# Decay products of a chunked state-space scan: the masked logs as a rounded part and a rest, multiplied in fp32r instead of fp32

## The chip, the cores and the metric

One core of one Trainium2 chip runs the whole kernel. The metric is device time in microseconds, median of three runs. Five compute queues matter here: TensorE (PE, with its weight loads shown apart as PEld), VectorE (DVE), ScalarE (ACT), GpSimd (POOL), and the SyncE queue (SP), which issues most DMAs.

## The reference, cut to what matters

The model is one layer of a hybrid decoder: an input projection, a Mamba-2 branch (chunked scan), a short-convolution branch, a merge, and a mixture of experts. The change touches one intermediate of the scan, the decay matrix of a chunk:

```python
acum = jnp.cumsum(dt * a_neg.reshape(G, R), axis=2)
causal = jnp.tril(jnp.ones((chunk, chunk), dtype=bool))
seg = acum[:, :, :, None] - acum[:, :, None, :]
decay = jnp.exp(jnp.where(causal[:, :, None, None], seg, -jnp.inf))
cb = jnp.einsum('bclgn,bcsgn->bclsg', Cm, Bm)
wts = cb[..., None] * decay * dt[:, :, None]
y_diag = jnp.einsum('bclsgr,bcsgrp->bclgrp', wts, x)
```

`seg[l, s]` is the sum of `dt*a` over the tokens s+1 to l. There are 32 heads in 4 groups of 8, and 592 tokens (528 of the prompt with its meta tokens, 64 of eight short sample sequences).

## The kernel before

The 592 tokens stand as five tiles: four of 128 tokens and one of 80 (16 prompt tokens and the 64 sample tokens). After the short-convolution branch and its projection, a loop over the 4 groups (`for g`) does the scan. Each turn of it has these stages.

**Convolutions.** PE multiplies blocks of `w_in` (`pe_block`, L570 to L588: 48 fp32r matmuls a block, on a rounded and a rest half of weights and activations, 264 and 328 columns in turn). ACT copies a block's result into `raw` (L1566, L1567), DVE convolves it (L1147, L1149) into `cv`, ACT applies SiLU (L1545). Six such tiles c = 0 to 5 per group. POOL writes history columns into `raw` (L1791), saves its tails (L1799, L1800), and makes the rest half of each weight block (`split_lo`, L1736) two blocks ahead of its use.

**Token tiles i = 0 to 4.** PE transposes x (L678), multiplies B and C (L681) and transposes B (L682). Then, for each half q of the group's heads (4 heads):

- POOL's `decays(i, q)` (L1812 to L1820) writes `rbuf[q]`: the 0/1 mask `m_le` (rows not after the column) times the log decays `da` of 4 heads, broadcast to 128 x 512 (80 x 320 for tile 4). It first waits until the product that read the same buffer is done (`p_seg`).
- PE multiplies it by the strict mask `m_gt` into PSUM bank `pS` (L691). The trace shows each of these fp32 instructions as two records. It has waited for `s_r` (POOL's operand) and `s_exp` (ACT has read the bank's last content), so the second half starts only after the first half's exp.
- ACT writes the exp of the bank to `wts` (L1581), DVE multiplies it by the masked B-C product (L1180, both operands in SBUF).

PE goes on with C times the state (L697), the output products of the eight heads (L747, which waits for both L1180), the state's increment (L753) and a transpose back (L773). Parts of three z-gate blocks (`pe_block` with `part=0` or `part=1`) fill PE between those steps in tiles 0, 1 and 2: part 1 of a block behind L697, part 0 of the next ahead of the second L691 of tiles 1 and 2. Tiles 3 and 4 have none.

**Tile 4** holds the sample sequences. DVE's order there is L1164 and L1165 (x times dt, from PSUM), L1168 (a copy of `sdec`, SBUF to SBUF, 80 x 512), L1172 (mask of the B-C product, from PSUM). PE's L702 waits for L1168 and, through `s_cb`, for L1172; behind it on PE stand the transposes of the sample states (L713), their products (L722, L729), and then L747. POOL's `bmask` product (L1839, two inputs in SBUF) waits for the group's last L691, because it overwrites `rbuf`. POOL's L1846 follows, gated by L713.

The order on each engine is written out by hand; semaphores link the engines. POOL's order around tile 0 is: tail of convolution tile 5, `decays(0, 0)`, `decays(0, 1)`, the `split_lo` for block 8 (used in tile 1), `decays(1, 0)` and so on.

`da` itself is made once, before the loop (L1128), and multiplied by the masks for the cumulated sums (L657 to L661).

Of the kernel before, what the change touches and what calls it, by code (L numbers as in the profile page):

```python
# [4 lines left out]
F32 = mybir.dt.float32  # L5
F32R = mybir.dt.float32r
# [53 lines left out]
def build(nc, ins, outs):  # L60
    ctx = ExitStack()
    with ctx:
# [3 lines left out]
        def sb(name, shape, dt=F32):  # L66
            return ctx.enter_context(nc.sbuf_tensor(name, shape, dt))[tuple(slice(None) for _ in shape)]
# [4 lines left out]

        ident = sb("ident", [P, P])
        m_le = sb("m_le", [P, P])
        m_gt = sb("m_gt", [P, P])
        ones = sb("ones", [P, P])
        R4 = ROWS[4]
        m_le4 = sb("m_le4", [R4, R4])
        m_gt4 = sb("m_gt4", [R4, R4])
        m_blk4 = sb("m_blk4", [R4, R4])  # L80
        eps = sb("eps", [P, 1])
        stat = sb("stat", [P, 4, TILES])
# [3 lines left out]
        xtail = sb("xtail", [P, XT_TILES, TAIL])  # L86
        stail = sb("stail", [P, 8, STAIL])
        dt_, da = sb("dt", [P, TILES, HEADS]), sb("da", [P, TILES, HEADS])
        e_acum, dte, dec = (sb(n, [P, TILES, HEADS]) for n in ("e_acum", "dte", "dec"))
        sdec = sb("sdec", [R4, HEADS])  # L90
        dg = sb("dg", [P, GK, 2])
# [20 lines left out]
        def carve(at, shape, area=area, size=AREA):  # L112
            n = 1
            for s in shape:
                n *= s
            v = area[:, at:at + n]
            assert at + n <= size, (at, n)
            if len(shape) == 2:
                v = v.rearrange("p (a b) -> p a b", a=shape[0])
            if len(shape) == 3:  # L120
                v = v.rearrange("p (a b c) -> p a b c", a=shape[0], b=shape[1])
            return v, at + n
# [12 lines left out]
        wdt, o = carve(o, [8, HEADS])  # L135
        dtb, o = carve(o, [HEADS])
        ea, o = carve(o, [HEADS])
        dtw, o = carve(o, [6, TILES * HEADS])

        s_c, so = carve(0, [2, T])  # L140
# [10 lines left out]
        bT, o = carve(o, [T])  # L151
        cT, o = carve(o, [T])
        sz, o = carve(o, [GK, T])
        raw, o = carve(o, [2, XPAD])
        h0T_more, _ = carve(o, [2, GW])
        cv, o = carve(o, [2, XPAD])
        rbuf, o = carve(o, [2, 4 * P])
        bmask, _ = carve(o - 8 * P, [NSEQ, NST])
        wts, o = carve(o, [2, 4 * P])
        rms, _ = carve(o, [T])  # L160
# [430 lines left out]
        def _(pe):  # L591
# [75 lines left out]
            with pe.Fori(0, GROUPS) as g:  # L667
# [4 lines left out]
                pe.wait_ge(s_rm, g + 1)  # L672
                for i in range(TILES):
                    r = ROWS[i]
                    le, gt = (m_le, m_gt) if i < 4 else (m_le4, m_gt4)

                    for k in range(GK):
                        m = nc.tensor.transpose(pT[0:r, k * P:(k + 1) * P], xT[:, k, tok(i)], ident[:, :])  # L678
# [5 lines left out]
                    for q in range(2):  # L684
                        if q == 1 and 1 <= i < 3:
                            pe_block(pe, g_block(g, 7 + i), 7 + i, hT_hi, hT_lo, part=0)
                        pe.wait_ge(s_r, g * 10 + (2 * i + q + 1))
                        pe.wait_ge(s_exp, g * 10 + (2 * i + q + 1))
                        if q == 0:
                            pe.wait_ge(s_st, g * 6 + (i + 1))  # L690
                        nc.tensor.matmul(pS[0:r, 0:4 * r], gt[0:r, 0:r], rbuf[0:r, q, 0:4 * r],  # L691
                                         start=True, stop=True).then_inc(p_seg, 1)

                    pe.wait_ge(s_cb, g * 5 + (i + 1))
                    pe.wait_ge(s_bt, g * 5 + (i + 1))
# [317 lines left out]
        def _(dve):  # L1013
# [78 lines left out]
            def o1_turn(f):  # L1092
                use, _, a, ause = o1_block(f, 1)
                dve.wait_ge(o_sg, f + 1)
                dve.wait_ge(w_done, use + 2)
                a0, a1 = acc_parts(acc[a])
                g0, g1 = halves(sg[:, 0, :])
                m0, m1_ = halves(mT[:, bass.ds(f, 1), :].rearrange("p a b -> p (a b)"))
                v.tensor_tensor(m0, a0, g0, ALU.mult)
                v.tensor_tensor(m1_, a1, g1, ALU.mult).then_inc(acc_free[a], 1)  # L1100
                dve.wait_ge(acc_free[a], ause + 2)
                dve.sem_inc(o_m, 1)
# [4 lines left out]
            for h, bank_ in ((0, pY), (1, pS)):  # L1107
# [19 lines left out]
            dve.wait_ge(s_dta, 3)  # L1127
            v.scalar_tensor_tensor(da[:, :, :], dt_[:, :, :], -1.0, ea.unsqueeze(1).broadcast_to([P, TILES, HEADS]),  # L1128
                                   ALU.mult, ALU.mult).then_inc(s_dtv, 1)
            o1_turn(1)  # L1130
            dve.wait_ge(s_dta, 5)
            link(v.tensor_tensor(dte[:, :, :], dte[:, :, :], dt_[:, :, :], ALU.mult))
# [571 lines left out]
        def _(pool):  # L1704
# [12 lines left out]
            def select(out, in_, pattern, base, mult, op=ALU.is_ge, fill=0.0):  # L1717
                link(gp.affine_select(out=out, in_=in_, pattern=pattern, compare_op=op, fill=fill, base=base,
                                      channel_multiplier=mult))

            select(ident[:, :], ident[:, :], [[-1, P]], 0, 1, ALU.not_equal, 1.0)
            select(m_le[:, :], m_le[:, :], [[1, P]], 0, -1)
            select(m_gt[:, :], m_gt[:, :], [[-1, P]], -1, 1)
            blk = m_blk4[:, 0:LASTP]
            select(blk, blk, [[0, LASTP]], LASTP - 1, -1)
            blk = m_blk4[:, LASTP:R4].rearrange("p (s c) -> p s c", c=SLEN)
            select(blk, blk, [[-SLEN, NSEQ], [0, SLEN]], -LASTP, 1)
            select(blk, blk, [[SLEN, NSEQ], [0, SLEN]], LASTP + SLEN - 1, -1)
            select(m_le4[:, :], m_blk4[:, :], [[1, R4]], 0, -1)
            gp.affine_select(out=m_gt4[:, :], in_=m_blk4[:, :], pattern=[[-1, R4]], compare_op=ALU.is_ge, fill=0.0,  # L1730
                             base=-1, channel_multiplier=1).then_inc(consts, 1)

            def split_lo(where, b, ahead=2):
# [52 lines left out]
            with pool.Fori(0, GROUPS) as g:  # L1786
                def history(c):
                    hold(pool, s_cvd, g * 6 + (c + 1))
                    f = bass.ds(conv_tile(g, c), 1)
                    rows = raw[:, c % 2, XH + TP:XPAD].rearrange("p (s c) -> p s c", c=XROW)  # L1790
                    gp.tensor_copy(rows[:, :, 0:XH], xvec[:, f, 5:29].rearrange("p a (s c) -> p (a s) c", c=XH)  # L1791
                                   ).then_inc(s_hist, 1)

                def tail(c):
                    _, _, a, ause = g_block(g, c)
                    hold(pool, acc_free[a], ause + 2)
                    f = bass.ds(conv_tile(g, c), 1)
                    rows = raw[:, c % 2, XH + TP:XPAD].rearrange("p (s c) -> p s c", c=XROW)
                    gp.tensor_copy(xtail[:, f, 0:XH].rearrange("p a b -> p (a b)"), raw[:, c % 2, TP:TP + XH])  # L1799
                    gp.tensor_copy(xtail[:, f, XH:TAIL].rearrange("p a (s c) -> p (a s) c", c=XH), rows[:, :, SLEN:XROW]  # L1800
                                   ).then_inc(s_tail, 1)

                history(0)
                history(1)
                for c in range(6):
                    if c >= 1:
                        split_lo(g_block(g, c), c)
                        if c < 5:
                            history(c + 1)
                    tail(c)  # L1810

                def decays(i, q):  # L1812

                    r = ROWS[i]
                    le = m_le if i < 4 else m_le4
                    hold(pool, p_seg, g * 10 + (2 * i + q + 1))
                    gp.tensor_tensor(rbuf[0:r, q, 0:4 * r].rearrange("p (h c) -> p h c", h=4),  # L1817
                                     le[0:r, 0:r].unsqueeze(1).broadcast_to([r, 4, r]),
                                     da[0:r, i, bass.ds(g * HPG + 4 * q, 4)].unsqueeze(2).broadcast_to([r, 4, r]),
                                     ALU.mult).then_inc(s_r, 1)  # L1820

                decays(0, 0)
                decays(0, 1)
                split_lo(g_block(g, 6), 6)
                for i in range(1, TILES):
                    for q in range(2):
                        decays(i, q)
                    if i < 4:
                        split_lo(g_block(g, 6 + i), 6 + i)
                    if i == 1:  # L1830

                        hold(pool, s_silu, g * 6 + 8)
                        gp.tensor_copy(cmask[:, 0:LASTP], cT[:, 4 * P:TP])
                        diag = cmask[:, R4 + LASTP:R4 + LASTP + NSEQ * (R4 + SLEN)].rearrange("p (s c) -> p s c", c=R4 + SLEN)
                        gp.tensor_copy(diag[:, :, 0:SLEN], cT[:, TP:T].rearrange("p (s c) -> p s c", c=SLEN)).then_inc(s_cm, 1)

                hold(pool, s_bt, g * 5 + 5)
                hold(pool, p_seg, g * 10 + 12)
                gp.tensor_tensor(bmask[0:R4], btok[0:R4, 0, :].unsqueeze(1).broadcast_to([R4, NSEQ, NST]),  # L1839
                                 m_blk4[:, LASTP:R4:SLEN].unsqueeze(2).broadcast_to([R4, NSEQ, NST]), ALU.mult  # L1840
                                 ).then_inc(s_bm, 1)

                hold(pool, s_df, g + 1)
                hold(pool, p_h0, g * 8 + 8)
                for k in range(GK):
                    gp.tensor_tensor(hs[:, k], hs[:, k], df[:, k, :].unsqueeze(2).broadcast_to([P, NSEQ, NST]), ALU.mult  # L1846
                                     ).then_inc(s_hd, 1)
                hold(pool, p_yb, g * 4 + 4)
                hold(pool, p_hs, g * 4 + 4)
                split_lo(g_block(g, 10), 10)  # L1850
# [113 lines left out]
```

## Time and profile before

| | |
|---|---|
| median of three runs | 1428.02 us (1427.01 to 1428.05) |
| the profiled execution | 1430.2 us, span 1428.5 us, mean granted PE clock 0.953 |
| PE busy | 1324.7 us, 93% of the span |
| DVE busy | 567.5 us, 40% |
| POOL busy | 457.0 us, 32% |
| ACT busy | 377.9 us, 26% |
| L691, PE | 80 records for 40 instructions, 39.1 us |
| L1817, POOL | 40 instructions, 41.1 us |

The times are of one profiled execution. A busy share is of the whole span; the kernel has stages with different limits, so what a step is worth is read from the stage that it stands in. The group loop runs from about 324 us to about 830 us; the experts' stage begins after 940 us.

### The profile page before, as it was taken

The page shows a single profiled execution, that of the slowest core. Times are in us where ns is not written, and L with a number is a line of the kernel's source. Part 1 is how long each engine was busy: PE and PEld are TensorE (multiplying, and loading weights), DVE is VectorE, ACT ScalarE, POOL GpSimd, SP SyncE. Part 2 cuts the span into 40 slices and gives each one's busy share as a digit, 9 for nine tenths or more (in the row PEclk, how much of TensorE's full clock was granted, in tenths as well). Part 3 has the DMA queues.
Part 4 walks back from the last instruction along what each step waited for, and adds up shares of the span by engine and source line. Part 5 has one row for each costly group of instructions (what it writes and reads, how often), then busy time and mean ns, then how long its engine had stood idle before and what let it go on. Part 6 is the DMA issues. An engine that isn't in the chain of part 4 may idle for free.

```text
span 1428.5 us, 23149 instructions
## 1 busy us (share of the span) xinstructions
PE 1324.7 (93%) x9087; PEld 1027.3 (72%) x9087; DVE 567.5 (40%) x816; ACT 377.9 (26%) x574; POOL 457.0 (32%) x380
## 2 busy tenths in 40 slices
PE   4999999999989999998999999999987999999990
PEld 4999999999759877975987799994474444444430
DVE  5444441026566754955676550011153111111115
ACT  4212124344234324333342531210121111101102
POOL 5444432345333533533252454330002112122110
PEclk8999999999989999999999999999956999999995
DMA  5223222235107303520631222337612999999925
GB/s 144 75 75 87 74 68 65 78 84 151 48 13 186 109 0 110 132 65 7 182 104 43 81 74 75 89 104 267 279 49 67 363 368 374 370 360 376 378 97 203
DMA packets 179334, 209.75 MB, mean 147 GB/s; under 512 B 12988, under 2 KB 154428, under 8 KB 170896
## 3 DMA queue, kind: packets, MB, share of 16 engines
q1 hardware_dynamic: 167970, 187.97, 40.2%
q10 hardware_dynamic: 4134, 11.11, 2.2%
q0 software_dynamic: 7168, 9.81, 1.9%
q8 instruction: 44, 0.72, 0.2%
q14 instruction: 18, 0.14, 0.0%
HBM read 196.93 MB, written 32.34 MB: 160 GB/s over the span
## 4 chain that ended last, share of the span: by engine, by line
PE 75%; DVE 12%; issue 4%; ACT 3%; DMA 3%; SPq 1%; DVEq 1%; ACTq 0%; POOLq 0%; POOL 0%
PE acc L584 36%; PE pT L944 8%; PE acc L819 5%; PE pS L957 4%; PE acc L983 4%; DVE area L1149 4%; PE pY L747 2%; PE pS L991 2%; PE pS L691 2%; DMA ring<-in_w_in 1%; PE acc L920 1%; PE acc L713 1%; DVE big L1220 1%; PE pY L927 1%; PE pS L753 1%
## 5 line engine op out<-in xcount | busy, mean ns | idle before, releaser
L584 PE MATMUL acc<-h_parts,ring_parts 128*128 128x328 f32 (+1 forms) x3840 | 551.5, 305 | 12.6 <-DVE h_parts L1047 6.9
L584 PEld LDWEIGHTS acc<-h_parts,ring_parts 128*128 128x128 f32 x3840 | 537.7, 192 | 29.0 <-issue 28.2
L1736 POOL TENSOR_TENSOR ring_parts<-ring,ring_parts 128x1024 fp32r<-128x1024 f32 x104 | 263.2, 2531 | 419.3 <-ACT ring_parts L1468 419.3
L1468 ACT ACTIVATE ring_parts<-ring 128x1024 fp32r<-128x1024 f32 x104 | 110.0, 1058 | 371.1 <-PE acc L584 353.6
L944 PE MATMUL pT<-area,big 128*64 128x512 f32 x384 | 116.1, 611 | 0.2 <-ACT big L1665 0.2
L584 PE MATMUL acc<-u_parts,ring_parts 128*128 128x264 f32 (+1 forms) x640 | 109.4, 299 | 0.0
L584 PEld LDWEIGHTS acc<-u_parts,ring_parts 128*128 128x128 f32 x640 | 96.4, 188 | 0.0
L1149 DVE SCALAR_TENSOR_TENSOR area<-area,xvec 128x616 f32<-128x616 f32 x72 | 90.1, 1252 | 10.5 <-DVE area L1147 0.6
L944 PEld LDWEIGHTS pT<-area,big 128*64 128x64 f32 x384 | 35.5, 140 | 78.8 <-issue 78.8
L584 PE MATMUL acc<-area_parts,ring_parts 128*128 128x264 f32 (+1 forms) x512 | 91.1, 299 | 0.0
L584 PEld LDWEIGHTS acc<-area_parts,ring_parts 128*128 128x128 f32 x512 | 78.4, 188 | 0.0
L1890 POOL DMA_INDIRECT big<-h_rows,gid_main x16 | 16.7, 1043 | 161.9 <-DVE big L1351 107.6
L957 PE MATMUL pS<-area,big 128*32 128x256 f32 x768 | 58.5, 381 | 0.0
L983 PE MATMUL acc<-area,big 128*64 128x512 f32 x192 | 58.4, 598 | 0.0
L944 PE MATMUL pT<-ring,big 128*64 128x512 f32 x128 | 56.6, 595 | 0.0
L1677 ACT ACTIVATE big<-pT 128x256 f32<-128x256 f32 x16 | 6.1, 384 | 190.3 <-PE pT L944 190.3
L1817 POOL TENSOR_TENSOR area<-m_le,da 128x512 f32<-128x512 f32 (+1 forms) x40 | 41.1, 1031 | 47.1 <-PE pS L691 47.1
L1911 POOL DMA_INDIRECT y_tok<-big,sid_over x16 | 16.0, 998 | 125.1 <-DMA y_tok<-big,sid_main 125.1
L1240 DVE TENSOR_TENSOR area<-acc,area 128x528 f32<-128x528 f32 x8 | 5.7, 707 | 115.7 <-PE acc L584 115.7
L1382 DVE TENSOR_TENSOR big<-big,pT 128x256 f32<-128x256 f32 x16 | 6.7, 421 | 111.5 <-ACT big L1677 111.5
L691 PE MATMUL pS<-area,m_gt 128*128 128x512 f32 (+1 forms) x80 | 39.1, 570 | 12.8 <-ACT area L1581 12.8
L1180 DVE TENSOR_TENSOR area<-area 128x512 f32<-128x512 f32 (+1 forms) x40 | 35.8, 903 | 32.3 <-ACT area L1581 30.8
(332 smaller groups left out, 1708.5 us busy)
## 6 DMA issues: line engine op xcount, KB each, us to landing
ring<-in_w_in SPq DMA_DIRECT2D x80, 512.0 KB, 4.1
area<-in_w_gate SPq DMA_DIRECT2D x24, 1024.0 KB, 6.3
area<-in_w_up SPq DMA_DIRECT2D x24, 1024.0 KB, 9.3
area<-in_w_down SPq DMA_DIRECT2D x24, 1024.0 KB, 11.5
area<-in_state_ssm SPq DMA_DIRECT2D x16, 512.0 KB, 7.0
out<-area SPq DMA_DIRECT2D x16, 512.0 KB, 5.3
ring<-in_w_ssd_out SPq DMA_DIRECT2D x16, 512.0 KB, 4.2
ring<-in_w_gate SPq DMA_DIRECT2D x8, 1024.0 KB, 11.5
```

Source lines behind the costliest of these rows:

```text
L584: m = nc.tensor.matmul(acc[a][:, h, 0:n], w[s][:, k, :], x[:, k, h * HALF:h * HALF + n], start=first and k == 0 and w is w_hi and x is hi, ...
L691: nc.tensor.matmul(pS[0:r, 0:4 * r], gt[0:r, 0:r], rbuf[0:r, q, 0:4 * r], start=True, stop=True).then_inc(p_seg, 1)
L747: m = nc.tensor.matmul(pY[0:r, h * HD:(h + 1) * HD], wts[0:r, h // 4, (h % 4) * r:(h % 4 + 1) * r], xdt[0:r, i % 2, h * HD:(h + 1) * HD], ...
L819: m = nc.tensor.matmul(acc[n % 4 // 2][0:ROWS[i], n % 2, :], mT[:, k, tok(i)], wo[h][:, k, :], start=k == 0, stop=k == 7)
L944: m = nc.tensor.matmul(pT[main_of(j), :], xT_[:, k, main_of(j)], gate_up_w(2 * p + j, k), start=k == 0, stop=k == 7)
L957: m = nc.tensor.matmul(pS[over_of(q), 0:FE], xT_[:, k, at:at + OVER], wexp[(2 * p + j) % 4][n][:, k, :], start=k == 0, stop=k == 7)
L983: m = nc.tensor.matmul(acc[1][main_of(j), h, :], hT_main[:, ft, main_of(j)], wexp[(2 * p + j) % 4][2][:, ft, h * 512:(h + 1) * 512], start ...
L1149: x = v.scalar_tensor_tensor(o_, raw[:, c % 2, n:n + XCONV], w[:, 0, n:n + 1], o_, ALU.mult, ALU.add)
L1180: v.tensor_tensor(w, w, cbm[0:r, 0:r].unsqueeze(1).broadcast_to([r, 4, r]), ALU.mult).then_inc(s_w, 1)
L1468: a_.activation(w_hi[b % 2], w_raw[b % 2], ACT.Copy).then_inc(hi_done, 1)
L1736: gp.tensor_tensor(w_lo[b % 2], w_raw[b % 2], w_hi[b % 2].bitcast(F32), ALU.subtract).then_inc(lo_done, 1)
L1817: gp.tensor_tensor(rbuf[0:r, q, 0:4 * r].rearrange("p (h c) -> p h c", h=4), le[0:r, 0:r].unsqueeze(1).broadcast_to([r, 4, r]), da[0:r, i, ...
```

## The change

The operand `rbuf` becomes two fp32r operands. POOL multiplies the mask by `da` and writes it as fp32r (`r_hi`, the place of `rbuf`), and multiplies it by `da_lo`, the rest of `da` over its fp32r rounding (`r_lo`, in columns of `raw`). PE adds two fp32r products with an fp32r mask `m_gtr` in the place of one fp32 product. `da_lo` is made by two DVE instructions of 160 columns, once. For tile 0 the two low products wait for the group's convolutions, since `r_lo` lies in `raw`.

```diff
-        m_gt = sb("m_gt", [P, P])
+        m_gtr = sb("m_gtr", [P, P], F32R)
...
-                        pe.wait_ge(s_r, g * 10 + (2 * i + q + 1))
+                        pe.wait_ge(s_r, g * 20 + (4 * i + (2 * q + 2 if i else q + 3)))
                         pe.wait_ge(s_exp, g * 10 + (2 * i + q + 1))
...
-                        nc.tensor.matmul(pS[0:r, 0:4 * r], gt[0:r, 0:r], rbuf[0:r, q, 0:4 * r],
-                                         start=True, stop=True).then_inc(p_seg, 1)
+                        nc.tensor.matmul(pS[0:r, 0:4 * r], gt[0:r, 0:r], r_hi[q][0:r, 0:4 * r], start=True, stop=False)
+                        nc.tensor.matmul(pS[0:r, 0:4 * r], gt[0:r, 0:r], r_lo[q][0:r, 0:4 * r], start=False, stop=True
+                                         ).then_inc(p_seg, 1)
...
+            dve.wait_ge(s_dtv, 3)
+            link(v.tensor_copy(da_hi, da[:, :, :]))
+            v.tensor_tensor(da_lo[:, :, :], da[:, :, :], da_hi.bitcast(F32), ALU.subtract)
             o1_turn(1)
...
-                def decays(i, q):
+                HIGH, LOW = [(r_hi, da)], [(r_lo, da_lo)]
+
+                def decays(i, q, parts):
...
-                    gp.tensor_tensor(rbuf[0:r, q, 0:4 * r].rearrange("p (h c) -> p h c", h=4),
+                    for part, d in parts:
+                        gp.tensor_tensor(part[q][0:r, 0:4 * r].rearrange("p (h c) -> p h c", h=4),
...
-                decays(0, 0)
-                decays(0, 1)
+                decays(0, 0, HIGH)
+                decays(0, 1, HIGH)
+                hold(pool, s_cvd, g * 6 + 8)
+                hold(pool, s_tail, g * 6 + 8)
+                decays(0, 0, LOW)
+                decays(0, 1, LOW)
                 split_lo(g_block(g, 6), 6)
                 for i in range(1, TILES):
                     for q in range(2):
-                        decays(i, q)
+                        decays(i, q, HIGH + LOW)
```

## Rows read from the trace of the kernel before

**Rows 1.** Waits of PE, 320 to 830 us: in total, times, longest.

```profile
PE pS L691 <- ACT area L1581: 12.8, 12, 1.8
```

**Rows 2.** Busy time by engine in the stretch of group 1, clock, DMA.

```profile
440.90:566.00 125.10, 116.44 (x763) 97.50 (x762) 80.19 (x107) 45.74 (x76) 50.33 (x46) 0.99 0.32 88
```

**Rows 3.** Timeline, group 1, PE in tile 1: start, length, engine, line, records.

```profile
500.12 1.02 PE L691 MATMUL pS<-area,m_gt 128*128 128x512 f32 x2
500.98 1.02 PE L697 MATMUL pO<-area 128*128 128x512 f32 x2
...
505.45 1.89 PE L747 MATMUL pY<-area 128*128 128x64 f32 x16
```

**Rows 4.** Timeline, group 1, POOL in tile 1.

```profile
497.64 1.04 POOL L1817 TENSOR_TENSOR area<-m_le,da 128x512 f32<-128x512 f32 x1 [1.29 <-PE pS L691]
```

**Rows 5.** Timeline, group 1, last convolution and tile 0.

```profile
479.63 2.42 DVE L1149 SCALAR_TENSOR_TENSOR area<-area,xvec 128x616 f32<-128x616 f32 x2
...
484.12 1.02 PE L691 MATMUL pS<-area,m_gt 128*128 128x512 f32 x2
484.19 2.35 POOL L1736 TENSOR_TENSOR ring_parts<-ring,ring_parts 128x1024 fp32r<-128x1024 f32 x1 [3.81 <-ACT ring_parts L1468]
...
484.91 1.28 ACT L1581 ACT_TABLE_LOAD   x1
...
486.94 1.10 PE L691 MATMUL pS<-area,m_gt 128*128 128x512 f32 x2 [1.80 <-ACT area L1581]
```

**Rows 6.** Timeline, group 1, tile 3.

```profile
522.55 1.02 PE L691 MATMUL pS<-area,m_gt 128*128 128x512 f32 x2
...
523.83 0.72 POOL L1817 TENSOR_TENSOR area<-m_le,da 80x320 f32<-80x320 f32 x1 [1.60 <-PE pS L691]
...
524.35 1.10 PE L691 MATMUL pS<-area,m_gt 128*128 128x512 f32 x2 [0.78 <-ACT area L1581]
524.73 0.69 DVE L1180 TENSOR_TENSOR area<-area 128x512 f32<-128x512 f32 x1
...
525.71 0.72 POOL L1817 TENSOR_TENSOR area<-m_le,da 80x320 f32<-80x320 f32 x1 [1.16 <-PE pS L691]
526.11 0.86 DVE L1180 TENSOR_TENSOR area<-area 128x512 f32<-128x512 f32 x1 [0.69 <-ACT area L1581]
...
527.07 1.97 PE L747 MATMUL pY<-area 128*128 128x64 f32 x16 [0.77 <-issue]
```

**Rows 7.** Timeline, group 1, tile 4.

```profile
532.39 0.74 PE L691 MATMUL pS<-area,m_gt 80*80 80x320 f32 x2 [0.61 <-ACT area L1581]
532.93 0.41 DVE L1168 COPY area<-sdec 80x512 f32 x1
...
533.31 1.91 POOL L1839 TENSOR_TENSOR area<-area,m_blk 80x1024 f32<-80x1024 f32 x1 [6.89 <-PE pS L691]
533.55 1.06 PE L702 MATMUL pT<-ident,area 80*128 80x8 f32 x8 [0.42 <-DVE area L1172]
```

**Rows 8.** Timeline, narrow windows: DVE and POOL overlapping, twice.

```profile
307.65 2.12 DVE L1138 COPY dg<-dnv 128x8 f32 x1 [0.51 <-DVE big L1100]
...
307.31 2.40 POOL L1736 TENSOR_TENSOR ring_parts<-ring,ring_parts 128x1024 fp32r<-128x1024 f32 x1 [2.78 <-ACT ring_parts L1468]
...
477.91 1.57 DVE L1149 SCALAR_TENSOR_TENSOR area<-area,xvec 128x616 f32<-128x616 f32 x1
...
477.79 1.04 POOL L1817 TENSOR_TENSOR area<-m_le,da 128x512 f32<-128x512 f32 x1
```

**Rows 9.** L713 in groups 1 and 2; the stretch 661 to 662 us.

```profile
534.46 1.94 PE L713 MATMUL acc<-ident,area 128*128 128x128 f32 x16
...
659.57 3.60 PE L713 MATMUL acc<-ident,area 128*128 128x128 f32 x16
...
661.00:662.00 1.00, 1.00 (x7) 1.00 (x6) 0.07 (x1) 0.74 (x2) 0.00 (x0) 0.50 0.00 0
```

**Rows 10.** Timeline, DVE, the step behind the decay logs.

```profile
222.61 0.71 DVE L1099 TENSOR_TENSOR big<-acc,area 128x528 f32<-128x528 f32 x1 [6.24 <-PE acc L584]
```

More of the change, by code:

```diff
@@ L78, in build @@
         m_le4 = sb("m_le4", [R4, R4])
-        m_gt4 = sb("m_gt4", [R4, R4])
+        m_gtr4 = sb("m_gtr4", [R4, R4], F32R)
+        m_gt, m_gt4 = m_gtr.bitcast(F32), m_gtr4.bitcast(F32)
         m_blk4 = sb("m_blk4", [R4, R4])
@@ L88, in build @@
         dt_, da = sb("dt", [P, TILES, HEADS]), sb("da", [P, TILES, HEADS])
+        da_lo = svec.rearrange("p a b -> p (a b)").rearrange("p (i h) -> p i h", h=HEADS)
         e_acum, dte, dec = (sb(n, [P, TILES, HEADS]) for n in ("e_acum", "dte", "dec"))
@@ L137, in build @@
         ea, o = carve(o, [HEADS])
+        da_hi = area_parts[:, o:o + TILES * HEADS].rearrange("p (i h) -> p i h", h=HEADS)
         dtw, o = carve(o, [6, TILES * HEADS])
@@ L153, in build @@
         sz, o = carve(o, [GK, T])
+        r_lo = [area_parts[:, o + XPAD * q + 5 - q:o + XPAD * q + 5 - q + 4 * P] for q in range(2)]
         raw, o = carve(o, [2, XPAD])
@@ L156, in build @@
         cv, o = carve(o, [2, XPAD])
-        rbuf, o = carve(o, [2, 4 * P])
+        r_hi = [area_parts[:, o + 4 * P * q:o + 4 * P * (q + 1)] for q in range(2)]
+        o += 8 * P
         bmask, _ = carve(o - 8 * P, [NSEQ, NST])
@@ L674, in _ @@
                     r = ROWS[i]
-                    le, gt = (m_le, m_gt) if i < 4 else (m_le4, m_gt4)
+                    gt = m_gtr if i < 4 else m_gtr4
                     for k in range(GK):
@@ L1722, in _ @@
             select(m_le[:, :], m_le[:, :], [[1, P]], 0, -1)
-            select(m_gt[:, :], m_gt[:, :], [[-1, P]], -1, 1)
+            select(m_gtr[:, :], m_gt[:, :], [[-1, P]], -1, 1)
             blk = m_blk4[:, 0:LASTP]
@@ L1729, in _ @@
             select(m_le4[:, :], m_blk4[:, :], [[1, R4]], 0, -1)
-            gp.affine_select(out=m_gt4[:, :], in_=m_blk4[:, :], pattern=[[-1, R4]], compare_op=ALU.is_ge, fill=0.0,
+            gp.affine_select(out=m_gtr4[:, :], in_=m_blk4[:, :], pattern=[[-1, R4]], compare_op=ALU.is_ge, fill=0.0,
                              base=-1, channel_multiplier=1).then_inc(consts, 1)
@@ L1816, in decays @@
                     hold(pool, p_seg, g * 10 + (2 * i + q + 1))
-                    gp.tensor_tensor(rbuf[0:r, q, 0:4 * r].rearrange("p (h c) -> p h c", h=4),
-                                     le[0:r, 0:r].unsqueeze(1).broadcast_to([r, 4, r]),
-                                     da[0:r, i, bass.ds(g * HPG + 4 * q, 4)].unsqueeze(2).broadcast_to([r, 4, r]),
-                                     ALU.mult).then_inc(s_r, 1)
-                decays(0, 0)
-                decays(0, 1)
+                    for part, d in parts:
+                        gp.tensor_tensor(part[q][0:r, 0:4 * r].rearrange("p (h c) -> p h c", h=4),
+                                         le[0:r, 0:r].unsqueeze(1).broadcast_to([r, 4, r]),
+                                         d[0:r, i, bass.ds(g * HPG + 4 * q, 4)].unsqueeze(2).broadcast_to([r, 4, r]),
+                                         ALU.mult).then_inc(s_r, 1)
+                decays(0, 0, HIGH)
[4 more added lines that the diff above has]
+                decays(0, 1, LOW)
                 split_lo(g_block(g, 6), 6)
```

## The prediction, made before the changed kernel was run

> **What bounds the kernel now.** I read the busy shares first, then the stages by windows, then PE's waits in the group loop, and last the timeline of one group, because every edit but one lies in that loop. A turn of the loop takes about 125 us and PE is busy 116 of it [rows 2]; in its token tiles PE runs nearly without a gap, so what it saves there comes off the time, while the convolutions are a chain of DVE's that starts at the end of the turn before and moves with it. PE's only large wait at the changed line is for the exp of the first half of the heads: 12.8 us in 12 times, which are tiles 0, 3 and 4 of four groups [rows 1]. Tiles 1 and 2 have a z-gate block between the two L691 and do not wait. All of this lies in group 1 as in the other three, to within some hundredths of a microsecond until L702; I give group 1 and multiply by four.
>
> **PE's work at L691.** The pair of records holds PE for 500.98 - 500.12 = 0.86 us [rows 3]. For fp32r, the z-gate block between L697 and L747 gives the cadence: its 24 matmuls of 328 columns run from 500.98 + 0.86 = 501.84 to 505.45, 0.150 us each [rows 3]; that is 328 columns at 2.4 GHz (0.137) and 0.013 more, with a weight load for each. So 512 columns cost 0.213 + 0.013 = 0.226, the pair of products 0.45, and each L691 of 512 columns gets shorter by 0.40 us. In tile 4 the fp32 pair streams 320 columns in 0.53 us (the same 1.67 ns a column), the fp32r pair in 2 x 0.147 less the last overhead = 0.28, so 0.25 less. Forty instructions save 32 x 0.40 + 8 x 0.25 = 14.8 us of PE's work; what follows is how much of it arrives.
>
> **Tile 0: 0.4 us a group.** The first L691 (484.12) gains nothing: its exp follows a table load that runs from 484.91 to 486.19 whatever PE does [rows 5]. The second one (486.94) is followed by PE work without a gap: 0.40. The low products wait for the last convolution, which ends at 479.63 + 2.42 = 482.05; with an estimated 0.3 us from semaphore to start the one that PE waits for is there at 482.35 + 1.04 = 483.4, ahead of 484.12 [rows 5]. That cover is 0.7 us. Behind them on POOL stands the `split_lo` that started at 484.19 [rows 5]; the second low product ends at 484.4, so it moves 0.2 us, and its block is needed in tile 1 after 496 us.
>
> **Tiles 1 and 2: 0.8 us each.** PE is never idle there, so both L691 count: 4 x 0.40 = 1.6 us. POOL now has two products of 1.04 us in place of one; it starts the ones for tile 2 at 497.64, 12 us before they are used, with a gap behind them until 501.40 [rows 4]. What they delay on DVE (L1180 in tiles 1 and 2) has over 2 us of slack before L747.
>
> **Tile 3: 0.4 us, between -0.1 and 1.0.** Here L691, exp, L691, exp, L1180, L747 is one chain, and by itself it would give 0.8. But POOL and DVE exclude each other on SBUF, as the next part shows, and POOL's work doubles here. Shifted: the first L691 ends 0.4 earlier, so POOL's two products for tile 4 run from 523.43 (was 523.83) to 524.87. DVE's first L1180, ready at 524.73, gets through at 524.88 and ends at 525.42, as before (524.73 + 0.69) [rows 6]. POOL's next product is ready at 524.92, waits for it, and runs to 526.0; the second L1180, ready at 525.3, streams behind it and ends at 526.56 against 526.97. L747 starts 0.1 later, so at 526.66, 0.4 earlier than 527.07 [rows 6]. If DVE gets in first it is 1.0, if both products go ahead of it -0.1.
>
> **Tile 4: minus 1.6 us.** This is where the chain turns. L691 is not on the path here: L702 waits for DVE's L1164, L1165, L1168, L1172 [rows 7], which hang on the tile before, so the saved 0.5 us of PE brings nothing. But they release `bmask` (L1839) earlier. The second L691 starts 0.25 earlier and is 0.25 shorter, so L1839 starts at 533.31 - 0.51 = 532.80. DVE's L1168 starts at 532.93 [rows 7]. Before, the copy was 0.38 us ahead; now POOL is 0.13 us ahead, for 1.91 us.
> What that costs is in two pairs of rows. A copy of 8 columns took 2.12 us where a POOL product (307.31 + 2.40 = 309.71) had started before it and ended 0.06 before its end; and an L1149 that started at 477.91, 0.12 us after a POOL product of the very kind of the change (477.79 + 1.04 = 478.83), ended at 479.48, its 616 columns after the product's end [rows 8]. So the later one waits for the whole instruction, and a lead of 0.12 us has decided. L1168 would stream from 532.80 + 1.91 = 534.71 to 534.98, 1.64 us after its present end of 533.34, and L702 and everything behind it move by as much. Bounds: 0 (the copy first) and 1.7. I take 1.64 by the nearest row, the L1149 with a lead of 0.12.
> The page "SBUF — State Buffer" of the Trainium skill, section "Who interferes with whom", has the same: an exclusive lock, held for the whole instruction by whoever issues first. The other reading of a slow DVE row would be that both go on at a reduced rate (the copy at a third of its rate: 1.2 us in place of 0.41, and a loss of 0.8 a group); by that reading the sum below would be 3.4 us better, by the page it stands.
>
> **The clock.** The state transposes behind L702 took 1.94 us in group 1 and 3.60 in group 2, where the granted clock was 0.50, the lower level of 1.2 GHz [rows 9]; groups 0 and 2 have such a passage there, groups 1 and 3 not, 1.66 us each. The longer idle time of PE ahead of them (from about 532.5 to 535.2) can bring it to the others. Bounds: -3.3 us (gone from two groups) to +3.3 (in all four). I take one group more, +1.66, since what precedes a fall is idle time and there is now more of it.
>
> **What costs nothing.** The two DVE instructions for `da_lo` (160 columns) stand after the `s_dtv` step that PE waits for and before an `o1_turn` for which DVE waits 6.24 us in the trace [rows 10]; without that cover, below 1 us once, or up to 2.4 behind a POOL product as in [rows 8]. The mask in fp32r is written by the same instruction. The semaphore counts double without further instructions. Groups are coupled through DVE, the SP queue (state stores, then the next weight block) and ACT; all of them start from the end of tile 4, so a shift there passes on whole. The experts' loads start after all of it and move with it.
>
> **The sum.** Per group 0.4 + 1.6 + 0.4 - 1.64 = 0.76 us less, 3.0 us in four, and 1.66 given back to the clock: 1.4 us less. The profiled execution took 1430.2 us (span 1428.5), so it would take 1428.8; the median shown is 2.2 us below the profiled one, so the time to expect is 1428.0 - 1.4 = 1426.6 us.
>
> **The rivals.** *The copy goes first (0.27).* If L1168 takes its ports before L1839, nothing is lost in tile 4 and the gain is 2.4 a group, 9.6 us: 1418.4. For it: the margin of 0.13 us is a difference of worked-out times, and L1168's start overlaps the end of L1165, so it may ask earlier than its start. Against: the row with a lead of 0.12.
> *The clock takes more than is saved (0.17), the slower side.* Mechanism: PE idles 2.7 us ahead of L713 in each group, the clock falls there each time and stays low through the state products (L722) as well. Price: 1.66 in each of the two groups without it now, and about as much again in each group for the second half of that stage: 3.3 + 6.6 - 3.0 = 6.9 at the most, 3 to 4 if only some of it: about 1432. It decides as soon as the clock costs more than 0.76 us a group on average above today. For it: PE's gap grows from 0.6 + 0.4 to 2.7 us. Against: in group 1 gaps of the same stage passed at full clock. The page "TensorE: Matmul & The Clock Gate" of the Trainium skill, section "What's actually happening", says that the clock is granted by how busy PE has recently been. By that rule a longer gap speaks for the fall in each group, the 3.3 to 6.6 us above; the trace agrees as far as two groups of four fall there today.
> *The pair is no cheaper (0.08).* If the second product's weight load is not hidden, or fp32r gains little at 512 columns, L691 stays near 0.8, L1839 keeps its place behind the copy, and POOL's double work costs nothing on the path: 1428. Against it: the cadence of 0.150 contains such a load.
>
> **How the numbers follow.** The forecast has 0.48, with its own range of 1423.3 to 1429.9 (the clock term from -3.3 to +3.3). This kernel's measurement can tell about 0.2%, 2.9 us, from no change: faster is below 1425.2, slower above 1430.9. Of the forecast's 0.48, 0.20 lie below, 0.26 between and 0.02 above; the copy first is 0.27 faster; the clock 0.02 same and 0.15 slower; no cheaper pair 0.07 same and 0.01 slower. That makes 0.47, 0.35, 0.18. The range that holds 8 in 10 reaches to the copy's case and into the clock's: 1417.8 to 1431.8.
>
> **What would show it.** Right: L691 pairs of 0.45 us between starts; tile 0's second L691, tiles 1 and 2 each shorter by 0.4 an instruction; L1168 of some 2.0 us in place of 0.41 in all four groups, with L1839 starting 0.1 before it, and a PE wait at L702 that grows by 1.6 us; L1180's second instance in tile 3 ending 0.4 earlier. Wrong: L1168 still at 0.41 with L1839 behind it (then 1418); a first L691 of tile 0 that waits for POOL; a `split_lo` that PE waits for in tile 1; L713 at 3.6 us in all groups, or L722 at twice its length (then the clock).

## The result: 1435.0 us, slower by 0.6%

Five runs of the changed kernel have a median of 1435.0 us (1434.14 to 1437.29), five of the kernel before 1428.05. The ratio is 1.0058 with a 95% interval of 1.0047 to 1.0069. The forecast was 1426.6 us with a range of 1417.8 to 1431.8, and the chance given to slower was 0.18: the time lies outside, on the side that I held least likely. The profiled execution took 1434.14 us (span 1432.4) against 1430.2 (1428.5). These two differ by 3.9 us only, since the first is the fastest of its five and the second is above all five of the kernel before; the stretches below tell where the time goes, the medians how much it is.

The waits of PE in the group loop (in total, times, longest) name the place at once. The wait for L1181, the B-C mask product, was 1.7 us in the kernel before and is 10.3 now; the one at the changed line has hardly moved from 12.8 [rows 1]:

```profile
PE pS L696 <- ACT area L1590: 13.2, 12, 2.1
PE pT L708 <- DVE area L1181: 10.3, 4, 2.6
```

Lines have moved: L691 is L696 and L697 now, L1168 is L1177, L1172 L1181, L1839 L1855, L702 L708, L713 L719, L747 L753, L793 L799.

Tile 1 of group 1 in the timeline, against [rows 3]: the two products of one half start 0.23 us apart and hold PE for 500.02 - 499.55 = 0.47 us, where one fp32 product took 0.86:

```profile
499.55 0.39 PE L696 MATMUL pS<-area_parts,m_gtr 128*128 128x512 f32 x1
499.78 0.40 PE L697 MATMUL pS<-area_parts,m_gtr 128*128 128x512 f32 x1
500.02 1.02 PE L703 MATMUL pO<-area 128*128 128x512 f32 x2
...
504.49 1.89 PE L753 MATMUL pY<-area 128*128 128x64 f32 x16
```

Tile 4 of group 1 in the timeline, against [rows 7]: POOL's L1855 starts 0.18 us ahead of DVE's copy, which lasts 2.01 us (before: 0.41) and ends 0.28 us after it. L708 then waits 2.58 us, and the state transposes behind it take 3.65 us, as they did in group 2 of before [rows 9].

```profile
529.90 0.37 PE L696 MATMUL pS<-area_parts,m_gtr 80*80 80x320 f32 x1 [0.52 <-ACT area L1590]
530.11 0.30 PE L697 MATMUL pS<-area_parts,m_gtr 80*80 80x320 f32 x1
...
530.60 1.91 POOL L1855 TENSOR_TENSOR area<-area,m_blk 80x1024 f32<-80x1024 f32 x1 [5.21 <-PE pS L697]
530.78 2.01 DVE L1177 COPY area<-sdec 80x512 f32 x1
532.72 0.23 DVE L1181 TENSOR_TENSOR area<-pO,m_le 80x80 f32<-80x80 f32 x1
533.00 1.68 PE L708 MATMUL pT<-ident,area 80*128 80x8 f32 x8 [2.58 <-DVE area L1181]
534.53 3.65 PE L719 MATMUL acc<-ident,area 128*128 128x128 f32 x16
```

And tile 0 of group 2, which had no counterpart before. Between the halves PE now idles 2.10 us (1.80 before, [rows 5]), and right behind that the granted clock is 0.50: the 24 products of the z-gate block take 5.45 us, in group 1 of the same execution 4.19. The second fence is a row of windows (stretch; its length; busy time of PE, PEld, DVE, ACT, POOL; granted clock; DMA).

```profile
614.47 0.50 PE L696 MATMUL pS<-area_parts,m_gtr 128*128 128x512 f32 x1 [2.10 <-ACT area L1590]
614.81 0.39 PE L697 MATMUL pS<-area_parts,m_gtr 128*128 128x512 f32 x1
615.04 1.78 PE L703 MATMUL pO<-area 128*128 128x512 f32 x2
...
615.83 5.45 PE L589 MATMUL acc<-h_parts,ring_parts 128*128 128x328 f32 x24
```

```profile
616.00:617.00 1.00, 1.00 (x3) 0.48 (x3) 1.00 (x1) 0.00 (x0) 1.00 (x2) 0.50 0.84 209
```

Measured from the starts of the same instructions, a group divides into stretches. Columns: tile 0; tiles 1 and 2 (each); tile 3; tile 4's first transpose to L702 or L708; from there to tile 4's L747 or L753 ("state stretch"); from there to the first product of the norm (L793, L799). Microseconds, groups 0 / 1 / 2 / 3.

| kernel | tile 0 | tiles 1, 2 | tile 3 | to L702 | state stretch | to the norm |
|---|---|---|---|---|---|---|
| before | 12.31 / 12.29 / 12.28 / 12.27 | 13.10 | 8.61 | 3.16 | 10.97 / 9.33 / 10.99 / 9.33 | 18.25 / 15.98 / 17.44 / 16.00 |
| changed | 13.44 / 11.83 / 13.43 / 14.47 | 12.33 | 8.18 | 4.76 | 11.00 / 12.56 / 11.01 / 10.96 | 17.45 / 16.32 / 17.43 / 18.19 |

The steps that do not depend on the clock are the same in all groups: -0.46 (tile 0 at full clock, 11.83), -0.77 twice, -0.43 and +1.60, in sum -0.83 us a group, -3.3 us. The stretches that vary carry the rest. Over the shortest value of each column, tile 0 costs 5.8 us more in the four groups together, the state stretch 8.2 (before 3.3) and the last column 5.5 (before 3.7): 19.5 against 7.0, 12.5 us more. -3.3 + 12.5 = 9.2; the last group's reciprocal of the norm starts at 825.34 us in place of 816.58, 8.8 later (the convolutions between the groups took 0.5 us less). What comes after it (gates, mixing, experts) took 4.9 us less in this execution (1432.4 - 825.34 = 607.1 against 611.9).

Windows of both kernels, over the loop from tile 0 of group 0 and over the part behind it, in the same columns as above. First the kernel before:

```profile
355.00:811.45 456.45, 424.17 (x2692) 347.84 (x2693) 283.98 (x397) 163.28 (x265) 178.38 (x154) 0.97 0.30 84
816.58:1428.50 611.92, 558.58 (x3919) 340.35 (x3917) 149.12 (x268) 99.31 (x150) 128.80 (x104) 0.93 0.61 228
```

Then the changed one:

```profile
355.00:820.20 465.20, 423.66 (x2693) 357.10 (x2693) 298.99 (x397) 164.08 (x266) 228.72 (x194) 0.94 0.30 83
825.34:1432.40 607.06, 554.03 (x3919) 336.76 (x3917) 149.13 (x268) 99.27 (x150) 128.77 (x104) 0.94 0.62 230
```

The granted clock of the loop fell from 0.97 to 0.94. Since the levels are 1.0 and 0.5, a mean of 0.97 is an estimated 27 us of the 456 at the lower one, and 0.94 some 56 us of the 465: 28 us more, and the 12.5 us lost are a little under half of that. Behind the loop PE has the same instructions in both, and the clock went the other way, 0.93 to 0.94, an estimated 13 us less at the lower level; that is enough for the 4.9 us. Why the clock was higher there is not shown. Over whole executions the mean granted clock was 0.945 to 0.949 in all five of the changed kernel and 0.953 to 0.959 in those of the kernel before that were measured beside the experiments.

### The profile page after: what moved, and what is told of

It is laid out like the page before. It is cut to its first block, busy times and chain, and to the rows that moved or that the text cites. A ratio compares the mean times of both kernels' runs of the same rounds, so it can differ in the third digit from the quotient of the medians.

```text
span 1432.4 us, 23263 instructions
## 1 busy us (share of the span) xinstructions
PE 1319.3 (92%) x9087; PEld 1032.7 (72%) x9087; DVE 582.7 (41%) x818; ACT 378.4 (26%) x574; POOL 508.0 (35%) x420
## 4 chain that ended last, share of the span: by engine, by line
PE 74%; DVE 13%; issue 4%; ACT 3%; DMA 3%; SPq 1%; DVEq 1%; ACTq 0%; POOLq 0%; POOL 0%
PE acc L589 36%; PE pT L950 8%; PE acc L825 5%; PE pS L963 4%; PE acc L989 4%; DVE area L1158 4%; PE pY L753 2%; PE pS L997 2%; DMA ring<-in_w_in 1%; PE acc L719 1%; PE acc L926 1%; PE pO L703 1%; DVE big L1229 1%; PE pY L933 1%; PE pS L759 1%
## 5 line engine op out<-in xcount | busy, mean ns | idle before, releaser
L1829 POOL TENSOR_TENSOR area_parts<-m_le,da 128x512 fp32r<-128x512 f32 (+1 forms) x40 | 44.5, 1117 | 23.0 <-PE pS L697 23.0
L1829 POOL TENSOR_TENSOR area_parts<-m_le,svec 128x512 fp32r<-128x512 f32 (+1 forms) x40 | 48.3, 1213 | 8.4 <-DVE area L1158 8.4
L1189 DVE TENSOR_TENSOR area<-area 128x512 f32<-128x512 f32 (+1 forms) x40 | 41.7, 1062 | 16.7 <-ACT area L1590 15.2
```

What stands on the lines that cost most here:

```text
L1189: v.tensor_tensor(w, w, cbm[0:r, 0:r].unsqueeze(1).broadcast_to([r, 4, r]), ALU.mult).then_inc(s_w, 1)
L1829: gp.tensor_tensor(part[q][0:r, 0:4 * r].rearrange("p (h c) -> p h c", h=4), le[0:r, 0:r].unsqueeze(1).broadcast_to([r, 4, r]), d[0:r, i, ...
```

## The experiments

The kernel before was measured beside each set of them (medians 1427.38, 1427.12 and 1427.47 us), and every ratio is to it. The stretches given are those of one profiled execution of each kernel. Two theories at first. A: the 1.6 us in tile 4 are POOL's lead at the shared ports, and the rest of the loss is PE's low clock, brought by the emptier stretches. B: GpSimd's doubled work is the cost wherever it stands.

### The copy ahead of bmask

```diff
                 hold(pool, s_bt, g * 5 + 5)
+                hold(pool, s_dx, g + 1)
                 hold(pool, p_seg, g * 10 + 12)
```

> The changed kernel with one wait more: POOL's bmask product starts only after DVE's copy of sdec. Theory A (POOL takes the shared ports 0.2 us ahead of the copy and holds them for its 1.9 us; the rest of the loss is TensorE's low clock): the stretch from tile 4's first transpose to L708 falls from 4.76 to about 3.2 us in each group, the copy from 2.01 to 0.41 us, 6.4 us less by this alone; the state transposes run at full clock in two groups again, 3 to 5 us more; the low clock of tile 0 stays. 1424 to 1429 us. Rival B (GpSimd's doubled work as such slows DVE, whatever its order): 1433 to 1435.

Measured: 1422.41 us (1420.37 to 1426.26), ratio 0.9970 [0.9959, 0.9982]: one wait more makes the changed kernel faster than the one before, 1.6 us below the range that I expected. To L708 it is 3.16 us in all groups again; state stretch 10.92 / 9.33 / 10.92 / 9.34; tile 0 13.46 / 13.42 / 11.84 / 13.44. The timeline of group 2:

```profile
652.88 0.41 DVE L1177 COPY area<-sdec 80x512 f32 x1
...
653.50 1.06 PE L708 MATMUL pT<-ident,area 80*128 80x8 f32 x8 [0.98 <-DVE area L1181]
653.64 1.91 POOL L1856 TENSOR_TENSOR area<-area,m_blk 80x1024 f32<-80x1024 f32 x1 [6.14 <-DVE area L1177]
```

The gain over the changed kernel, 12.6 us by the medians, is twice the 6.4 of the copy alone: part of the low clock behind it goes too (5.0 us in the four state stretches, 1.9 in the four behind them).

### GpSimd's work without PE's, and PE's without GpSimd's

First both products on GpSimd, with PE's one fp32 product of before. `r_f` is the place of `r_hi`, written and read as fp32, and the mask is `m_gt` again.

```diff
-                        nc.tensor.matmul(pS[0:r, 0:4 * r], gt[0:r, 0:r], r_hi[q][0:r, 0:4 * r], start=True, stop=False)
-                        nc.tensor.matmul(pS[0:r, 0:4 * r], gt[0:r, 0:r], r_lo[q][0:r, 0:4 * r], start=False, stop=True
-                                         ).then_inc(p_seg, 1)
+                        nc.tensor.matmul(pS[0:r, 0:4 * r], gt[0:r, 0:r], r_f[q][0:r, 0:4 * r],
+                                         start=True, stop=True).then_inc(p_seg, 1)
```

> GpSimd as in the changed kernel (both products, the low ones unused; the high ones written as fp32), TensorE with the one fp32 product of before. Theory A: GpSimd's second product is hidden, the last L696 ends where it did, so bmask stays behind the copy (0.41 us) and no tile changes by more than 0.3 us: 1427 to 1430 us. Rival B: 1432 or more. For tile 0 theory A also says that the clock stays high there, since TensorE's work in it is as before.

Measured: 1427.33 us (the median of eleven, one of which took 5387.58 us), ratio 0.9999 [0.9988, 1.0010]. The copy stands 0.32 us ahead of bmask and takes 0.42 us, tile 0 12.23 in all groups, tile 3 8.55. Twice the products on GpSimd cost nothing. Timeline, group 1:

```profile
532.16 0.42 DVE L1177 COPY area<-sdec 80x512 f32 x1
...
532.48 1.91 POOL L1855 TENSOR_TENSOR area<-area,m_blk 80x1024 f32<-80x1024 f32 x1 [5.70 <-PE pS L697]
```

The reverse: PE with two fp32r products, GpSimd with one. Both products read the high operand, so this kernel leaves the rest of the logs out of its results.

```diff
-                        pe.wait_ge(s_r, g * 20 + (4 * i + (2 * q + 2 if i else q + 3)))
+                        pe.wait_ge(s_r, g * 10 + (2 * i + q + 1))
...
-                        nc.tensor.matmul(pS[0:r, 0:4 * r], gt[0:r, 0:r], r_lo[q][0:r, 0:4 * r], start=False, stop=True
+                        nc.tensor.matmul(pS[0:r, 0:4 * r], gt[0:r, 0:r], r_hi[q][0:r, 0:4 * r], start=False, stop=True
...
-                hold(pool, s_cvd, g * 6 + 8)
-                hold(pool, s_tail, g * 6 + 8)
-                decays(0, 0, LOW)
-                decays(0, 1, LOW)
...
-                        decays(i, q, HIGH + LOW)
+                        decays(i, q, HIGH)
```

> TensorE as in the changed kernel (two fp32r products), but both on the high operand, so GpSimd makes one product as before; the rest part of the decays is left out of the sum. Theory A: tiles 1 and 2 at 12.33 us, bmask still ahead of the copy (2.0 us, L708 1.6 us late), low clock in tile 0 of some groups: 1432 to 1436 us, like the changed kernel. Rival B (GpSimd's doubled work is the loss): 1419 to 1424.

Measured: 1436.51 us, ratio 1.0067 [1.0054, 1.0080], as slow as the changed kernel. Tile 0 11.90 / 14.54 / 11.89 / 13.52, to L708 4.82 us, state stretch 12.62 / 10.96 / 12.57 / 11.00. Timeline, group 1; the lead of POOL is 0.12 us here and decides as well:

```profile
535.00 1.91 POOL L1851 TENSOR_TENSOR area<-area,m_blk 80x1024 f32<-80x1024 f32 x1 [6.39 <-PE pS L697]
535.12 2.06 DVE L1177 COPY area<-sdec 80x512 f32 x1
```

With these two, theory B has fallen: the whole loss comes with PE's faster products and none with GpSimd's work.

### Tile 0 in fp32

```diff
+                        if i in FP32_TILES:   # (0,)
+                            nc.tensor.matmul(pS[0:r, 0:4 * r], gt[0:r, 0:r].bitcast(F32), r_f[q][0:r, 0:4 * r],
+                                             start=True, stop=True).then_inc(p_seg, 1)
+                            continue
...
-                decays(0, 0, HIGH)
-                decays(0, 1, HIGH)
...
-                decays(0, 0, LOW)
-                decays(0, 1, LOW)
+                decays(0, 0, ONE)
+                decays(0, 1, ONE)
```

> The changed kernel, but tile 0 keeps the one fp32 product and GpSimd's one operand; tiles 1 to 4 as changed. Theory A: tile 0 takes 12.3 us in all four groups (changed: 11.83 at full clock, 13.44 or 14.47 in three groups with the low clock), no low clock in it; tile 4 stays at 4.76 us. By tile 0 alone 3.6 us less: 1430 to 1433. If the low clock in tile 0 is chance and not TensorE's shorter work there, it shows up in some groups all the same and the time stays at 1434 to 1437.

Measured: 1434.71 us, ratio 1.0058 [1.0043, 1.0072]: a miss for the time, though tile 0 did what was expected (12.22 / 12.24 / 12.22 / 12.23, no low clock). The state stretch rose to 12.01 / 12.47 / 12.57 / 11.98. So PE's shorter work in tile 0 does bring its clock down, but keeping it up there left more of the low clock in tile 4 of this execution, and the time as it was. The same with the ordered bmask on top:

> Both repairs together: bmask waits for the copy, and tile 0 keeps the fp32 product. From the first repair's trace (1422.4 us; tile 0 at 13.46, 13.42, 11.84, 13.44 us) theory A says: tile 0 at 12.23 in all groups, 3.2 us less, 1418 to 1421. If tile 0's shorter work is not what lowers the clock there, 1422 to 1424, since the saved 0.4 us a group is lost.

Measured: 1423.66 us (1417.42 to 1427.53), ratio 0.9963 [0.9946, 0.9981], not below the ordered bmask alone: a miss. Tile 0 12.22 in all groups, state stretch 9.34 / 10.92 / 12.57 / 12.57.

### Filling PE's idle time

The next kernels give PE products of 264 columns whose results nobody reads.

```diff
+                        pe.wait_ge(acc_free[0], g * 5 + 26)
+                        pe.wait_ge(acc_free[1], g * 5 + 26)
+                        for k in range(18):
+                            nc.tensor.matmul(acc[0][:, 0, 0:HALF], hT_hi[:, k % 8, 0:P], hT_hi[:, k % 8, 0:HALF],
+                                             start=True, stop=True)
                         pe.wait_ge(s_xd, g * 5 + 5)
```

> The changed kernel, and behind the last L697 of each group TensorE multiplies 18 blocks of 264 columns into a free bank (2.2 us, results unused), inside the 2.6 us in which it waits for the blocked copy. Theory A1 (the long idle time there is what lowers the clock behind it): L708 comes no later (4.76 us from tile 4's first transpose), but the stretch from L708 to tile 4's L753 takes 9.3 us in all four groups (changed: 11.0, 12.6, 11.0, 11.0), 8 us less, 1425 to 1429. Rival C (the clock falls there by chance, or by the small products behind it): 1433 to 1437, with stretches of 11 us still in two or more groups.

Measured: 1443.01 us, ratio 1.0107 [1.0090, 1.0124], far above the 1425 to 1429 expected. Here I had put the products in the wrong place, behind PE's wait for L1181 (`s_cb`), so they followed the idle time instead of filling it. It still tells something (timeline, group 1):

```profile
535.97 3.78 PE L708 MATMUL acc<-h_parts 128*128 128x264 f32 x18 [2.76 <-DVE area L1186]
539.55 1.18 PE L713 MATMUL pT<-ident,area 80*128 80x8 f32 x8
540.59 1.94 PE L724 MATMUL acc<-ident,area 128*128 128x128 f32 x16
```

The 18 products took the low clock (3.6 us from start to start, for 2.2 at full clock) and the transposes behind them ran in 1.94 us; the state stretch is 9.45 or 9.46 us in all four groups. What is low is what follows the idle time, here fp32r products of 264 columns and in the changed kernel transposes. Then the same 18 ahead of that wait (`if i == 4`, before the waits for `s_cb` and `s_bt`):

> As the filled run of before, but the 18 products stand ahead of the waits for L1181, so TensorE runs them while the copy is blocked. Theory A1: tile 4's first transpose to L708 4.8 us, L708 to L753 9.3 us in all groups (changed: 11.0, 12.6, 11.0, 11.0); tile 0 still at 13.4 in some groups. 8 us less than the changed kernel: 1426 to 1430. Rival C (the clock falls there whatever TensorE does just ahead): 1433 to 1437.

Measured: 1427.56 us, ratio 1.0010 [0.9999, 1.0021]. The copy is still blocked (2.02 us, to L714 4.77), but the state stretch is 9.33 / 9.34 / 9.34 / 9.34. Timeline, group 1:

```profile
529.24 2.38 PE L704 MATMUL acc<-h_parts 128*128 128x264 f32 x18
...
529.59 1.92 POOL L1861 TENSOR_TENSOR area<-area,m_blk 80x1024 f32<-80x1024 f32 x1 [5.21 <-PE pS L697]
529.77 2.02 DVE L1183 COPY area<-sdec 80x512 f32 x1
...
531.99 1.06 PE L714 MATMUL pT<-ident,area 80*128 80x8 f32 x8 [0.37 <-DVE area L1187]
532.91 1.95 PE L725 MATMUL acc<-ident,area 128*128 128x128 f32 x16
```

Useless work, 8.7 us an execution, makes the kernel 7.4 us faster. With 17 more between the halves of tile 0:

> The last run, and 17 such products more between the halves of the heads in tile 0, where TensorE idles 2.1 us. If the low clock is the whole rest of the loss: tile 0 at 11.8, L708 to L753 at 9.3 us in all groups, the groups' sum of low-clock stretches no larger than in the kernel before; then only the copy's 1.6 and the tiles' 2.4 us a group are left: 1420 to 1425. If low clock passes only move elsewhere, 1428 or more.

Measured: 1425.71 us, ratio 0.9990 [0.9979, 1.0001]; tile 0 11.84 / 11.83 / 11.84 / 11.84, state stretch 9.34. Just above the expected 1420 to 1425: the column to the norm holds 17.28 / 17.52 / 17.43 / 18.19 now, 6.5 us over its best (4.0 with tile 4 filled alone), so part of the low clock stands there instead. The kernel before with such products (15 and 3) is the control:

> The kernel before with 15 such products in tile 0 and 3 in tile 4. Its tile 0 never falls to the low clock, its state stretch does in two groups (11.0 against 9.3 us): 1.7 to 3.3 us less if the filling prevents that, 1424 to 1427; the same as before, 1427 to 1429, if three products are too few.

Measured: 1425.73 us, ratio 0.9991 [0.9980, 1.0002]; state stretch 9.34 in all groups (before 10.97 / 9.33 / 10.99 / 9.33); its interval contains 1. And with the ordered bmask (17 and 8 products):

> bmask waits for the copy, tile 0 filled with 17 products, tile 4 with 8 (its idle time is 1.0 us there). Theory A: tile 0 at 11.8 and the state stretch at 9.3 us in all groups, 8 us below the run with the ordered bmask alone (1422.4): 1413 to 1417. If the low clock only moves elsewhere: 1420 to 1424.

Measured: 1421.44 us (1413.69 to 1425.35), ratio 0.9945 [0.9923, 0.9967]. A miss: tile 0 is 11.84 and three state stretches 9.34, but in the profiled execution, the slowest of the seven, the low clock stands behind them: 17.43 / 18.25 / 18.21 / 18.26 to the norm, and 50.8 to 50.9 us from there to the next group's tile 0, where the ordered bmask alone took 48.8 to 49.1. Three of the seven executions (1413.69 to 1415.73) do lie in the expected range, so one kernel's low passages do not lie alike in all its executions.

### The z-gate block moved

Part 1 of the z-gate block 7 goes between the halves in tile 0, ahead of the second L696, in place of behind L703. First with the ordered bmask, then in the kernel before.

```diff
+                        if q == 1 and i == 0:
+                            pe_block(pe, g_block(g, 7), 7, hT_hi, hT_lo, part=1)
...
-                    if i < 3:
+                    if 1 <= i < 3:
                         pe_block(pe, g_block(g, 7 + i), 7 + i, hT_hi, hT_lo, part=1)
```

> bmask waits for the copy, and in tile 0 the second part of the z-gate block stands between the two halves of the heads (where TensorE idles 2.1 us for the table load and the exp) in place of behind L703. Theory A: the idle time there goes, about 0.8 us of waiting for exp and L1189 comes behind L703, and the clock stays high in tile 0: 10.6 us in all four groups against 13.4 or 11.8; 1414 to 1419. Against it: if the wait ahead of L753 is as long as the one removed, tile 0 stays near 12 and the time near 1421.

> The kernel before with only the z-gate part moved as in the last run: tile 0 from 12.3 to about 11.1 us (1.8 us of idle time filled, some 0.7 new), 4 to 5 us less: 1422 to 1424. The difference to the last run is then what the fp32r products and the ordered bmask bring by themselves: 2.4 us by theory A in each group, 9.6, less what the clock takes in the state transposes.

Measured: 1419.39 us (1413.39 to 1424.28), ratio 0.9950 [0.9931, 0.9968], tile 0 10.98 / 12.49 / 10.97 / 10.97, state stretch 10.97 / 10.96 / 9.34 / 9.33, to the norm 18.23 / 18.15 / 18.00 / 17.46; and 1427.99 us, ratio 1.0005 [0.9995, 1.0016], tile 0 12.35 / 12.34 / 12.35 / 12.76. The second was a miss: 1422 to 1424 was expected. In its timeline the idle time reappears ahead of L749 (1.09 us) and of L775 (1.53 at its weight load), the latter behind L1192, which takes 2.23 us (0.68 before), since a `split_lo` now starts ahead of it: again DVE behind POOL.

```profile
489.41 2.40 POOL L1738 TENSOR_TENSOR ring_parts<-ring,ring_parts 128x1024 fp32r<-128x1024 f32 x1 [0.36 <-ACT ring_parts L1470]
...
490.12 2.23 DVE L1192 TENSOR_TENSOR area<-area,dec 128x512 f32<-128x512 f32 x1
```

The first of the two is the fastest version by median that beats both kernels, without wasted work; its interval overlaps those of the ordered bmask alone and of the filled kernel with the ordered bmask.

### Counted over all kernels

The fourteen profiled executions have four groups each. PE idles 2.10 to 2.19 us between the halves of tile 0 in five kernels (the changed one, the ordered bmask alone, one product on GpSimd, tile 4 filled behind and ahead of the wait): tile 0 has low clock in 14 of their 20 groups. It idles 1.70 to 1.80 us there in four (before, doubled GpSimd, the two with fp32 in tile 0): in none of 16; nor in any of the 12 groups of the three kernels with that time filled. Where the z-gate part was moved the gap is elsewhere and shorter (1.27 or 1.09 us), and one group of four fell in each all the same. The state stretch has low clock in all 12 groups of the three kernels in which PE waits for the blocked copy with nothing in between, in 11 of 24 where the copy is free and nothing was filled in, and in 1 of 16 where products stand ahead of that wait. So the length of PE's idle time changes how often a low passage follows, and does not settle it for a single group.

## Why the prediction was wrong

Point by point:

- **PE's work at L691**: right within 0.02 us (0.47 in place of 0.45 for the pair). Tiles 1 and 2 gave 0.77 each for the 0.80 expected.
- **Tile 0**: the 0.4 is there where the clock is full (11.83 in group 1). The low products end ahead of PE's need as expected; the first starts 0.43 us behind the last convolution in group 1, for the estimated 0.3. That tile 0 could fall to the low clock was not in my sum nor in any rival; it did in three of four groups, 5.8 us.
- **Tile 3**: 0.43 for 0.4, and the order was the one worked out: GpSimd's product and DVE's take turns, and the second L1180 (L1189 now) ends 0.44 us earlier, counted from the tile's first transpose.
- **Tile 4**: right in place, cause and size: POOL ahead by 0.18 us (0.13 expected), the copy at 2.01 us, 1.60 us lost a group for 1.64. The run with the ordered bmask and the two half changes show it.
- **The clock: this step failed.** I took "one group more, +1.66", with +3.3 as its upper bound, from one place, the state transposes. In the profiled execution the loop's low clock cost 12.5 us more than before: 5.8 in tile 0, 4.9 in the state stretch, 1.8 behind. By the medians, 7.0 us slower with 3.3 us saved in the steps that do not vary leave 10.3 us for it and for all else that the sum does not hold, against the 1.66 taken. The rival named the right mechanism and, for the state stretch, a longer fall (group 1 with 12.56), and called 1432 its time. Its most, 6.9 us slower, is the 7.0 that the medians show, but by luck: it put up to 9.9 us of low clock into the one stretch, where 4.9 came, and nothing into tile 0 and the part behind. The error was to price the low clock at one of the places where it had been seen (in the kernel before the column to the norm varies too, from 15.98 to 18.25), rather than at each place where the change shortens PE's work next to a wait. Tile 0 was such a place by my own working: the first L691 gains nothing there, so most of its saved 0.40 us becomes idle time (1.80 before, 2.10 now at the second L696).
- **What costs nothing**: the two DVE instructions for `da_lo` take 0.24 and 0.33 us, and DVE still waits 5.61 us behind them (6.24 before, [rows 10]). GpSimd's doubled work: shown by the run with it alone.

Shown: the blocked copy (six kernels with POOL ahead by 0.12 to 0.18 us and a copy of 2.00 to 2.07 us, eight with the copy ahead by 0.32 to 0.76 us and 0.41 or 0.42 us long), and that with PE's idle time filled the low clock behind it nearly goes from that stretch (the counts above). Open: in which of the stretches a low passage comes to lie, since a gap of the same 2.10 us was followed by one in some groups and not in others. In four kernels (tile 0 in fp32, both places filled, each with and without the ordered bmask) it stood in later stretches instead, and their times came out 0.7 to 4.4 us above the range expected. Open too is why the clock behind the groups was higher in the profiled execution.

## What to carry to other kernels

An operation made faster changes the order of everything that waits for it. Ask of each engine that it releases earlier what that engine will now start ahead of; here one wait between GpSimd and a small copy was worth 12.6 us by the medians. And where a saved matmul time turns into idle time next to a wait, it is not neutral: count such places over the whole loop and give each a price for the low clock, since together they can cost more than the saving.

## What the runs showed of the hardware

- A copy of 0.41 us between SBUF tiles waits for a whole GpSimd product of 1.91 us that started 0.12 to 0.18 us before it, and takes 2.00 to 2.07 us. This agrees with the rule that the prediction cites from the Trainium skill ("SBUF — State Buffer", "Who interferes with whom"); the reading of a reduced rate (1.2 us) is out. With the copy ahead by 0.32 us it took 0.42 us, and GpSimd's product its 1.91.
- Two fp32r products of 512 columns with 128 x 128 weights hold PE for 0.47 us, one fp32 product for 0.86.
- With low clock in it, tile 0 of the changed kernel took 1.6 us more than at full clock in two groups and 2.6 us more in a third; the state stretch took 1.6 to 1.7 us more, and 3.2 more in group 1.
- Products without use in PE's idle time gained more than their place in the queue cost: 7.4 us by medians in the changed kernel, 1.7 in the kernel before (the interval of its ratio contains 1, so that gain is not clear of the noise).
